# A hybrid mixer's second half in another order, and block products in four column groups

## The reference

```python
def compress_blocks(tok, pos, w1, b1, w2, n_cmp):        # n_cmp = 15
    idx = CMP_STRIDE * jnp.arange(n_cmp)[:, None] + jnp.arange(CMP_BLOCK)[None, :]
    blk = tok[:, idx] + pos[:, None, :]
    blk = blk.transpose(0, 1, 3, 2, 4).reshape(bsz, n_cmp, NSA_KV_GROUPS, CMP_BLOCK * NSA_HEAD_DIM)
    return jax.nn.gelu(blk @ w1 + b1) @ w2               # w1: 2048 x 256, for keys and for values

def hybrid_mixer(h, ...):
    z, xbc, dt_raw, q, k, v, f_raw = jnp.split(h @ w_in, offs, axis=-1)
    xbc = jax.nn.silu(causal_conv(xbc, conv_w, conv_b))
    xs, bm, cm = jnp.split(xbc, ...)
    dt = jax.nn.softplus(dt_raw + dt_bias)
    y = ssd_chunked(xh, dt, -jnp.exp(a_log), bm, cm) + d_skip * xh      # two chunks of 128 tokens
    y = y * jax.nn.silu(z)
    y_ssm = y * lax.rsqrt(mean of y*y per group of 512 + NORM_EPS) * ssm_norm_g
    log_f = jax.nn.log_sigmoid(f_raw + fox_b_f)
    o = forgetting_attention(q, k, v, log_f)                            # 8 heads of 128
    return jnp.concatenate([y_ssm, o], axis=-1) @ w_out
```

## Time and profile before

| | us |
|---|---|
| runs shown | 2211.20, 2202.96, 2211.48; median 2211.2 |
| profiled execution, own time | 2208.97 |
| its span | 2207.5 |
| PE busy | 2122.1 (96%) |
| DVE busy | 1365.1 (62%) |
| ACT busy | 1127.2 (51%) |
| POOL busy | 72.0 (3%) |
| DMA | 369.27 MB, mean 167 GB/s |

### The profile page before, as it was taken

How to read it: one execution, slowest core, us unless ns; L and a number is a source line. 1 busy time by engine, 2 the same in 40 slices (tenths; PEclk the granted TensorE clock), 3 DMA queues, 4 the chain that set the end, 5 groups by cost and what they waited for, 6 DMA issues and landing times.

```text
span 2207.5 us, 25418 instructions
## 1 busy us (share of the span) xinstructions
PE 2122.1 (96%) x9936; PEld 1736.3 (79%) x9936; DVE 1365.1 (62%) x1948; ACT 1127.2 (51%) x1818; POOL 72.0 (3%) x106
## 2 busy tenths in 40 slices
PE   8999899999999989999999999979999999999998
PEld 6877787888887778788788877658788788877887
DVE  5977655554797665555465447665655655577553
ACT  5547455443555546544454446534544544377442
POOL 0000100000000200000000000100000000010000
PEclk9999999999999999999999999989999999999999
DMA  6562353555555234345455544313555555544453
GB/s 236 193 216 89 121 181 122 189 187 177 189 191 191 80 131 154 139 184 191 172 189 184 190 181 172 129 43 115 193 181 189 190 183 189 190 177 165 178 187 133
DMA packets 52950, 369.27 MB, mean 167 GB/s; under 512 B 6207, under 2 KB 6463, under 8 KB 9312
## 3 DMA queue, kind: packets, MB, share of 16 engines
q1 hardware_dynamic: 49104, 356.54, 44.7%
q10 hardware_dynamic: 3216, 9.53, 1.4%
q0 software_dynamic: 512, 1.57, 0.4%
HBM read 366.31 MB, written 1.31 MB: 167 GB/s over the span
## 4 chain that ended last, share of the span: by engine, by line
PE 86%; DVE 6%; ACT 5%; issue 1%; DMA 0%; POOL 0%; ACTq 0%; DVEq 0%
PE ps L481 25%; PE ps L483 25%; PE ps L482 25%; PE ps L569 2%; DVE nT_lo L1243 2%; PE ps L620 1%; DVE ring_lo L1181 1%; PE ps L742 1%; PE ps L553 1%; PE ps L604 1%; ACT nT_hi L1975 1%; ACT upper_w L1911 1%; ACT ostage L1963 1%; PE ps L821 1%; PE ps L539 1%
## 5 line engine op out<-in xcount | busy, mean ns | idle before, releaser
L482 PE MATMUL ps<-ring_lo,nT_hi 128*128 128x512 f32 x1952 | 764.2, 392 | 0.0
L1181 DVE TENSOR_TENSOR ring_lo<-ring,upper_w 128x1024 fp32r<-128x1024 f32 x443 | 536.1, 1231 | 279.7 <-ACT upper_w L1911 276.9
L1911 ACT CAST upper_w<-ring 128x1024 fp32r<-128x1024 f32 x443 | 456.2, 1056 | 340.7 <-PE ps L483 170.8
L481 PE MATMUL ps<-upper_w,nT_hi 128*128 128x512 f32 (+1 forms) x1352 | 540.5, 400 | 19.0 <-DVE ring_lo L1181 11.5
L483 PE MATMUL ps<-upper_w,nT_lo 128*128 128x512 f32 (+1 forms) x1224 | 478.8, 391 | 0.0
L482 PEld LDWEIGHTS ps<-ring_lo,nT_hi 128*128 128x128 f32 x1952 | 370.9, 190 | 73.3 <-issue 0.5
L481 PEld LDWEIGHTS ps<-upper_w,nT_hi 128*128 128x128 f32 x1352 | 257.6, 191 | 78.6 <-issue 9.5
L483 PEld LDWEIGHTS ps<-upper_w,nT_lo 128*128 128x128 f32 x1224 | 232.1, 190 | 49.1
L482 PE MATMUL ps<-ring_lo,z_hi 128*128 128x512 f32 x624 | 242.9, 389 | 0.0
L483 PE MATMUL ps<-upper_w,tT_lo 128*128 128x512 f32 (+1 forms) x528 | 206.8, 392 | 0.0
L1181 DVE TENSOR_TENSOR ring_lo<-ring,PT_w 128x1024 fp32r<-128x1024 f32 x108 | 129.5, 1223 | 73.8 <-ACT PT_w L1911 73.1
(11 more groups left out here) (330 smaller groups left out, 2492.5 us busy)
## 6 DMA issues: line engine op xcount, KB each, us to landing
ring<-in_w SPq DMA_DIRECT2D x339, 1024.0 KB, 4.8
big<-in_gains ACTq DMA_DIRECT2D x7, 512.0 KB, 4.7
z<-in_mem ACTq DMA_DIRECT2D x2, 1024.0 KB, 5.1
big<-skew POOLq DMA_DIRECT2D x8, 192.0 KB, 7.0
x<-in_x SPq DMA_DIRECT2D x2, 512.0 KB, 4.9
xn<-in_w ACTq DMA_DIRECT2D x1, 1024.0 KB, 10.7
out<-x ACTq DMA_DIRECT2D x2, 512.0 KB, 2.7
const<-in_const ACTq DMA_DIRECT2D x1, 529.0 KB, 3.5
```

Source lines behind the costliest of these rows:

```text
L481: PE.matmul(out, hi, w_hi, start=start, stop=False)
L482: PE.matmul(out, hi, w_lo, start=False, stop=False)
L1181: V.tensor_tensor(ring_lo[:, q % RING, cols], ring[:, q % RING, cols], upper(n).bitcast(F32), ALU.subtract).then_inc(*lo_cut.up(h))
L1911: A.copy(upper(n), ring[:, q % RING, part * HALF:(part + 1) * HALF]).then_inc(*hi_cut.up(h))
```

## The change

- The four cmp chunks are no longer one segment behind in5: one is taken behind in3, one behind in4, two behind in5. In each the 8 matmuls go in turn to partitions 0, 32, 64 and 96 of bank 6, so four partial sums stand in four groups of 30 partitions, from four groups of columns of the array. ACT copies all 128 rows; `hidden` sums the groups with a stationary side of K = 128 and a moving matrix `fold` that DVE makes once a layer.
- The mean moves behind `block_scores`, the variance behind the last half of in6, taps 25 to 30 into the front and the halves of in6, the scaling into in7; ACT's Square and Sqrt move with them, and its copy of hid ahead of the scaling of in5.
- In the hybrid mixer x2 goes to banks 6, 7; the turn of the inputs is laid behind the first half of z0 and uses four banks; ACT's Exp of the step sizes goes ahead of its copies. Silu of z moves from behind z3 to behind z2. `to_rows` uses banks 6, 7, 5.
- Q and K of head group 0 are transposed in z7; those of group 1 with `within(1)` between the scores of fox0 and fox1. Key terms 0 come before the weighings on DVE, key terms 1 on POOL. Banks and buffers of y, S0, Q and K change so.
- ACT takes the squares of y in two pairs and scales the two groups of the first token tile, DVE those of the second. y is transposed behind fox0's value products through banks 0 to 3. The first three halves of out0 are laid behind fox1, fox2 and fox3; the transposes of the heads come behind them. All of fox's transposed weights are copied by ACT (`by_act`).

```diff
+CMP_AT = {3: (0,), 4: (1,), 5: (2, 3)}
...
+            for piece in CMP_AT.get(b, ()):
+                w.add(f"{l}.cmp{piece}", [at + 24 + piece], split=False)
         w.end_run(f"{l - 1}.in{LAST[0]}" if l else "0.in0", f"{l}.in{FIRST[-1]}")
-        w.add(f"{l}.cmp", range(at + 24, at + 28), split=False)
...
-    hid = S[0:30, 0, 0:2, :]
+    hid, fold = S[:, 0, 0:2, :], S[:, 1, 1, 0:30]
...
-    y_banks = ((5, 6), (4, 7))
+    key_banks = ((4, 5), (6, 7))
+    y_banks = ((6, 7), (4, 5))
...
-    row_sets = ((0, 4), (4, 4), (8, 2))
+    row_sets, row_banks = ((0, 4), (4, 4), (8, 2)), (6, 7, 5)
...
-            rows_in(3, (2, 3), {0: blocks})
-            rows_in(4, (0, 1))
-            rows_in(5, (2, 3))
...
+            def block_product(piece):
+                kind, cc = piece // 2, piece % 2
+                if piece == 0:
+                    PE.wait_ge(*dve_out.at(f"{l}.b.2"))
+                    free(6)
+                h = W.span[f"{l}.cmp{piece}"][0]
+                q = W.halves[h][0]
+                PE.wait_ge(*landed[q % RING].at(q))
+                w = ring[:, q % RING, :]
+                for j in range(8):
+                    o = 32 * (j % 4)
+                    m = PE.matmul(ps[o:o + 30, 6, kind * 256:(kind + 1) * 256], cmpb[:, kind, 8 * cc + j, :, :].rearrange("p g c -> p (g c)"),
+                                  w[:, j * 256:(j + 1) * 256], start=(cc == 0 and j < 4), stop=(cc == 1 and j >= 4))
+                    if j % 4 == 3:
+                        m.then_inc(*half_used.up(h + j // 4))
+
+            rows_in(3, (2, 3), {0: blocks})
+            block_product(0)
+            rows_in(4, (0, 1))
+            block_product(1)
+            rows_in(5, (2, 3))
+            block_product(2)
+            block_product(3)
...
-                        m = PE.matmul(ps[:, 7, o:o + 30], hid[:, kind, ht * P:(ht + 1) * P], ident[0:30, 0:30], start=True, stop=True)
+                        m = PE.matmul(ps[:, 7, o:o + 30], hid[:, kind, ht * P:(ht + 1) * P], fold, start=True, stop=True)
...
-            rows_in(6, (0, 1), {0: hidden, 1: lambda: (block_rows(), variance()), 2: block_scores})
+            rows_in(6, (0, 1), {0: hidden, 1: block_rows, 2: lambda: (block_scores(), mean()), 3: variance})
...
+                banks = (2 * b, 2 * b + 1) if b < 2 else (6, 7)
...
+                turn("hyb.cin", cols_of(z, H_X), 12, [act_out.at("hyb.x2")], lambda c: act_out.at(f"hyb.cin.{c}"), banks=(6, 7, 4, 5))
...
+                gemm(f"hyb.z{b}", lhs, banks, beside=lambda c: inputs() if b == 0 and c == 0 else None)
...
-                    b = 6 + (3 * t + q) % 2
+                    b = row_banks[q]
...
+                PE.wait_ge(*(pool_out if hg else dve_out).at(f"hyb.terms{hg}"))
+                free(*key_banks[hg])
...
-            work = {0: sums, 2: lambda: to_rows(0), 3: lambda: row_sums(0), 5: lambda: to_rows(1), 7: products, 8: lambda: row_sums(1), 15: lambda: key_sums(0)}
+                held(dve_out.at(f"hyb.added{hg}"), *key_banks[hg])
+
+            def queries(hg):
+                turn(f"hyb.Q{hg}", cols_of(z, H_Q + 512 * hg), 4, [act_out.at(f"hyb.z{2 + hg}")], lambda c: act_out.at(f"hyb.Q{hg}.{c}"))
+
+            def keys(hg):
+                turn(f"hyb.K{hg}", cols_of(z, H_K + 512 * hg), 4, [act_out.at(f"hyb.z{4 + hg}")], lambda c: act_out.at(f"hyb.K{hg}.{c}"))
+
+            work = {0: sums, 2: lambda: to_rows(0), 3: lambda: row_sums(0), 5: lambda: to_rows(1), 7: products, 8: lambda: row_sums(1),
+                    12: lambda: queries(0), 13: lambda: keys(0), 15: lambda: key_sums(0)}
...
-            within(1)
-
-            for hg in range(2):
-                turn(f"hyb.Q{hg}", cols_of(z, H_Q + 512 * hg), 4, [act_out.at("hyb.z7")] if hg == 0 else (), lambda c: act_out.at(f"hyb.Q{hg}.{c}"))
-                turn(f"hyb.K{hg}", cols_of(z, H_K + 512 * hg), 4, (), lambda c: act_out.at(f"hyb.K{hg}.{c}"))
-            key_sums(1)
...
+            def second_tokens():
+                within(1)
+                queries(1)
...
+            def out_halves(first, last):
+                for c in range(first, last):
+                    h = W.span["hyb.out0"][c]
+                    w_hi, w_lo = weights(h)
+                    for k in range(2):
+                        f, cols = 2 * c + k, slice(k * BLK, (k + 1) * BLK)
+                        PE.wait_ge(*dve_out.at(f"hyb.yT.lo{f}" if f < 8 else f"hyb.hT.lo{f - 8}"))
+                        for t in range(TT):
+                            m = three(ps[:, 2 * t, :], pair_hi(f, TOK[t]), wide_lo(f, TOK[t]), w_hi[:, cols], w_lo[:, cols], f == 0, f == 15)
+                    m.then_inc(*half_used.up(h))
+
+            def y_product():
+                free(0, 2)
+                out_halves(0, 1)
+            attention(fox_units(), scores, lambda i: [act_out.at(f"hyb.K{i // 2}.2"), act_out.at(f"hyb.Q{i // 2}.2")], between=second_tokens, first=lambda: key_sums(1), by_act=True,
+                      beside={0: lambda: parts("hyb.yT", cols_of(z), 8, lambda c: [act_out.at("hyb.ynorm"), dve_out.at("hyb.ynorm")], (0, 1, 2, 3)), 1: y_product, 2: lambda: out_halves(1, 2)})
+            out_halves(2, 3)
+            parts("hyb.hT", lambda c, t: heads_out[c // 4][t][:, c % 4 * P:(c % 4 + 1) * P], 8, lambda c: [dve_out.at("fox3.out")])
+            out_halves(3, 8)
...
+                if n == 0:
+                    V.tensor_reduce(fold, ident.rearrange("p (q i) -> p i q", q=4)[:, 0:30, :], AX_X, ALU.add).then_inc(*dve_out.up(f"{l}.fold"))
...
-            cuts(f"{l}.in5", lambda n: tap(22 + n))
...
+            cuts(f"{l}.in5", lambda n: tap(22 + n) if n < 3 else None)
+            cut_first(f"{l}.in6", 1)
+            tap(25)
+            cut_first(f"{l}.in6", 2)
+            tap(26)
+            tap(27)
+
+            def centre():
...
-            work = {1: lambda: (block_keys(), deviation()), 2: block_scores, 3: lambda: (scaled(), block_weights())}
-            cuts(f"{l}.in6", lambda n: work.get(n, lambda: None)())
-            cuts(f"{l}.in7", lambda n: block_values() if n == 3 else None)
+            work = {0: lambda: tap(28), 1: lambda: (block_keys(), tap(29), tap(30)), 2: lambda: (block_scores(), centre()), 3: lambda: (block_weights(), deviation())}
+            cuts(f"{l}.in6", lambda n: work[n]())
+            late = {0: scaled, 3: block_values}
+            cuts(f"{l}.in7", lambda n: late.get(n, lambda: None)())
...
-                    11: lambda: weigh(0), 12: lambda: weigh(1), 13: lambda: key_terms(0)}
+                    11: key_terms, 12: lambda: weigh(0), 13: lambda: weigh(1)}
...
+            def second_tokens():
+                V.wait_ge(*pool_out.at("hyb.dx1"))
+                own()
...
                 mean_square("hyb.y", 4, 512, 0)
...
+            def y_parts():
                 V.wait_ge(*pool_out.at("hyb.y.rstd"))
-                for i, s in enumerate(groups):
-                    V.tensor_scalar(s, s, st[:, i:i + 1], None, ALU.mult).then_inc(*dve_out.up("hyb.ynorm" if i == 3 else None))
-            attention(fox_units(), plain_out, first=y_norm, beside={1: lambda: lo_parts("hyb.yT", 8, (pair_hi, wide_lo), s2("ng"))})
-
-            def heads_beside(n):
-                if n == 2:
-                    lo_parts("hyb.hT", 8, ((lambda c: pair_hi(8 + c)), (lambda c: wide_lo(8 + c))))
-            cuts("hyb.out0", heads_beside)
+                for i in (2, 3):
+                    V.tensor_scalar(groups[i], groups[i], st[:, i:i + 1], None, ALU.mult).then_inc(*dve_out.up("hyb.ynorm" if i == 3 else None))
+            attention(fox_units(), plain_out, between=second_tokens, first=y_norm, by_act=True, amid={1: y_parts},
+                      beside={0: lambda: lo_parts("hyb.yT", 8, (pair_hi, wide_lo), s2("ng"), (0, 1, 2, 3)), 1: lambda: cut_ahead(span[0]), 2: lambda: cut_ahead(span[1])})
+            cut_ahead(span[2])
+            lo_parts("hyb.hT", 8, ((lambda c: pair_hi(8 + c)), (lambda c: wide_lo(8 + c))))
+            for h in span[3:]:
+                cut_ahead(h)
             for h in W.span["hyb.out1"][:-2]:
                 cut_ahead(h)
...
+            cuts(f"{l}.in5")
+            cut_first(f"{l}.in6", 2)
+            A.wait_ge(*product(f"{l}.cmp3"))
+            A.copy(hid, ps[:, 6, :].rearrange("p (k n) -> p k n", k=2)).then_inc(*act_out.up(f"{l}.hid"))
+            scaled(f"{l}.in5", block_of(z, 3), ps[:, 2:4, :], func=ACT.Sigmoid)
...
+            cut_to(W.halves[W.span[f"{l}.in6"][2]][2])
+            hidden()
+            rows_in(6, 0, block_of(z, 4), ACT.Sigmoid, {1: block_rows, 3: lambda: (squared(), block_weights())})
+            rows_in(7, 2, block_of(z, 5), ACT.Sigmoid, {0: deviation, 1: normed, 2: weights_turned})
...
-                scaled(f"hyb.x{b}", block_of(z, 2 + b), ps[:, 2 * (b % 2):2 * (b % 2) + 2, :])
+                bank = (0, 2, 6)[b]
...
             A.wait_ge(*dve_out.at("hyb.sp"))
             e = acc[:, 3, 0:56]
```

(35 more changed lines are left out.)

127 lines of the change are left out of this document (43 added, 84 removed).

## The result

The changed kernel takes 2174.6 us (median of four runs, 2172.6 to 2176.4) where the kernel before takes 2207.1 beside it: a ratio of 0.986 (95% interval 0.983 to 0.988). In a second comparison the two stood at 2174.6 and 2205.9, ratio 0.985 (0.983 to 0.988). The forecast was 2183 us, range 2172 to 2198. In the profiled executions the span fell from 2207.5 to 2171.1 us, by 36.4, more than the 28.1 of the sum; the medians of the runs differ by 32.5 and 31.2.

What follows compares the result with a forecast made beforehand. TensorE was taken as the bound (86% of the chain that ended last), VectorE next. Savings of 1.9 + 5.2 + 11.6 + 9.4 = 28.1 us from 2208.97 gave 2180.9, plus 2.2 for the median: 2183 us, range 2172 to 2198.

Steps and rivals of the forecast that it cites:

- A: Turning the hybrid mixer's inputs, laid behind the first products of z0: saves 1.9 us (bounds 0.5 and 2.5).
- B: z4 to z7 of the hybrid mixer: waits and half clock go, some wait returns; saves 5.2 us (bounds 2.0 and 7.2).
- C: End of z7 to the first output product: less idle and low clock; saves 11.6 us (bounds 5 and 18).
- D: Block products of both layers, in four column groups at once: saves 9.4 us (bounds 0 and 13).
- The walk through the queues: Tail behind z7: following four engine queues with old durations found 5.0 us of PE waits, taken as 7.
- my walk: Input projection: layer 0 followed step by step with PE's waits; 5.5 us saved a layer at 1.0 us a chunk.
- Column groups in turn: Rival for the block products: the groups do not run at once and gain nothing; 2192 us, chance 0.14.
- Loads that alternate with products: Rival for the block products: load and product take turns, 5.3 us a chunk; 2206 us, chance 0.03.
- C at half its gain: Rival for the tail behind z7: its serial chain shows again between the output halves; 2189 us, chance 0.16.
- the tail at half clock: Rival: PE, cut into short bursts, stays at half clock over the whole tail; 2220 us, chance 0.02.
- Rival 5: Whole kernel better than forecast, down to 2172 us, with the bounds at their good end; chance 0.05.

Runs made afterwards that it cites:

- before_again: The kernel before, unchanged, run once more for a second trace: 2206.9 us.
- triangle_later: The changed kernel with the second row sums asked for one half of products later: 2168.3 us, ratio 0.983.
- front_only: The kernel before with the input projection's part of the change alone: 2192.7 us, against 2201.0 for the kernel before beside it.
- hybrid_only: The kernel before with the hybrid mixer's part of the change alone: 2179.8 us, against 2201.0 for the kernel before beside it.
- second_first: The changed kernel with the second tokens put ahead of the first unit's scores on all engines: 2170.1 us.
- halves_behind: The changed kernel with the first three output halves behind the attention instead of between its steps: 2172.7 us.
- one_group: The changed kernel with all block products in one column group again, places kept: 2189.4 us.
- two_and_pairs: The changed kernel with layer 0's block products in two column groups, layer 1's in four with two in a row to each: 2178.0 us, one run.

## Why the prediction came out right, point by point

| step | forecast | profiled | what was off |
|---|---|---|---|
| A | 1.9 | 2.6 | the 24 transposes took 3.9 us, now 2.8 |
| B | 5.2 | 3.8 | half clock behind the new wait |
| C | 11.6 | 17.3 | low clock: 8.7 returned, not 3.2 |
| D | 9.4 | 7.8 | more saved, more waited |
| elsewhere | 0 | 4.9 | layer 0's half clock, its start |
| sum | 28.1 | 36.4 | |

A is read from the start of x0 to the sums (82.0 and 79.4 us), B from there to the end of z7 (59.9 and 57.9, less 1.8 for 16 transposes that have moved in), C from there to the transposes behind the output product (104.7 and 85.6, with the 1.8), D as P of both layers (3.4 and 4.4). Of the 4.9 elsewhere, 3.5 lie between P of layer 0 and P of layer 1, where before_again also takes 3.6 us less than the first trace of before: they are not the change's. The steps themselves gave 31.5 us.

**A.** The waits of 1.4 us and 0.5 us went as put down. I left the transposes at their cost, but a break for a bank costs more than its idle time, which the profile counts only from the end of the last record (0.27 us long). Their starts stand 0.109 us apart, and across the two breaks 0.57 and 0.46 us, where the idle times are 0.30 and 0.19. From the first transpose to the next product it was 3.63 us and is 2.53: 1.1 us less, of which 0.5 was in the sum. The clock had no part in it: it was 1.00 there (1331 to 1337 us) in the kernel before.

**B.** All waits went where the step had them, and the one that was to come did: 1.91 us for the second triangle, put down as 2.0. What failed is one term: I added 1.7 us for the half clock behind the old wait and charged none behind the new one. It was 1.8 us (5.40 for eight records of 3.59). With it the sum is 3.4. triangle_later confirms both halves of that loss, and shows that it could have been had for one number in a table.

**C.** The walk through the queues gave 7 us of waits, the trace has 6.8, though not the same ones. K1 waited 1.9 and not 0.6, as I had overlooked the squares of y that ACT does ahead of the copies. POOL's terms took 4.8 us (I took 5) and nobody waited for them. The scaled rows cost 1.3 and not 2.4 (the row for L572 names DVE's L1336, but that ended at 1456.90; ACT's scaling, L2392, ended at 1457.75, and PE went on at 1457.85). The first output half cost 1.5 for the parts of y and not 0.9 for a bank. The longest wait, 2.0 us ahead of the second unit's transposes, had not been seen. It has the same cause as K1's: its probabilities were ready at 1450.66, but the first unit's had to leave the banks, and ACT copies them only behind the second pair of squares:

```profile
1451.51 0.63 ACT L2375 ACTIVATE tT<-z 128x512 f32<-128x512 f32 x1
1452.13 0.56 ACT L2076 COPY PTs<-ps 128x512 f32<-128x512 f32 x1
```

The idle part is 8.6 by the forecast's 15.4 against 6.8, as counted (8.4). The clock is the mis-sized term: I put down 5.7 us lost before and 2.5 after. Before it was 8.7, by what is left of C's 17.3 without the idle part, and after it is nil (clock 1.00). Not in my list were both groups of L1031 (4.57 and 4.49 against 3.68) and some tenths in each of the other groups. The mean clock of 0.83 over 61 us gave the warning: worked out as in step B, it is some 21 us at half clock and up to 10 us lost. front_only shows that 3.4 us of this belong to how the tail happened to be met, so a fair size for C is 14 to 17 (an estimate from these two numbers). hybrid_only (H 232.8) shows that the whole of it comes with the hybrid part. Within it the halves were tested, 0.5 us, and they don't hold the clock up; which step brought the clock back stays open. That the idle time went because the key terms come ahead of the weighings, and because ACT took squares, scalings and the copies of the probabilities over from DVE, fits the waits that are gone, but no run shows it: second_first and halves_behind only rule out two other steps.

**D.** The products fell to 0.97 us a chunk, below my lower bound of 1.1 and my value of 1.4, so PE work fell by 10.1 us a layer and not 8.6 (the 0.97 is half of the 1.93 us of two chunks in a row). I had taken the bound from records of another kind and not from the simplest ratio, a quarter of the pitch. The waits behind were right in kind and nearly in size (keys 1.2 for 1.6, last tap 1.25 for 1.3, squares none for 0.8), but behind the wait for the tap the mean's products ran at half clock (3.5 us in layer 1 for 2.0), and a cut and the convolution's parts add 0.5 to 0.9. Layer 0 also waits 0.8 us for the block inputs ahead of the first chunk. At 1.0 us a chunk my walk had given 5.5 us a layer; 3.4 and 4.4 were measured. Here too the clock behind a wait was the missing term, and with it the switches between narrow and full products, below.

**The rivals.** Column groups in turn (2192) is refuted by one_group and two_and_pairs. Loads that alternate with products (2206) too: 14.3 us for 64 records in one group, 0.216 us from start to start, leave no room for loads of 0.1 us each. The Trainium skill, page "TensorE: Matmul & The Clock Gate", section "The mechanism", has a list by which loads overlap running products only where their row groups differ; by that sentence they should not have been hidden, as all use all rows, and the trace doesn't agree. The same section also lets a load be taken ahead into a background weight buffer; that would fit, and no run here tests it.

The prediction also passed over the drain at a change of tiling mode, which the Trainium skill states (page "TensorEngine Tiling (Array Packing)", section "Key Properties"), because the row of L742 has no idle before it. The idle column doesn't show it, but the starts do. Here is one chunk between full products in the changed kernel, then eight full products of the same 256 columns (L761) between the same neighbours:

```profile
119.60 0.39 PE L486 MATMUL ps<-upper_w,nT_lo 128*128 128x512 f32 x1
119.92 1.07 PE L743 MATMUL ps<-ring,PTs 128*30 128x256 f32 x16
120.92 0.50 PE L484 MATMUL ps<-upper_w,nT_hi 128*128 128x512 f32 x1
121.25 0.39 PE L485 MATMUL ps<-ring_lo,nT_hi 128*128 128x512 f32 x1
```

```profile
156.06 0.39 PE L486 MATMUL ps<-upper_w,nT_lo 128*128 128x512 f32 x1
156.29 1.89 PE L761 MATMUL ps<-cbuf,const 128*128 128x256 f32 x8
157.82 0.58 PE L484 MATMUL ps<-upper_w,nT_hi 128*128 128x512 f32 x1
158.24 0.40 PE L485 MATMUL ps<-ring_lo,nT_hi 128*128 128x512 f32 x1
```

Into the narrow products it is 0.32 us where 0.23 is usual. From the first of them to the second full one behind it is 1.33 us, where four distances of 0.216 and one of 0.227 make 1.09. For L761 it is 1.95 us, just eight of 0.216 and one of 0.227. So a switch there and back costs some 0.3 us here. The trace thus agrees with the page. The layer has three such pairs, and before the change it had two and not one, as the mean stood between chunks 3 and 4: the change adds some 0.3 us a layer (an estimate from these starts).

C at half its gain (2189) did not happen, nor the tail at half clock (2220): its clock is 1.00. Rival 5, the good end of the bounds (2172), had a chance of 0.05, and the measured 2174.6 lies nearer to it than to the forecast of 2183, because C came out near its upper bound of 18.

**The measured time** lies 8.4 us below the forecast. Half of that is the start: I counted from a median of 2211.2, and the kernel before took 2207.1 in this comparison. The gain is 32.5 us for 28.1. It is that near partly by luck, since errors of both signs met: C's clock (5.5 us) and D's products (1.5 us a layer) gave more than I put down, and the clock behind two new waits, which I had put at nothing, took some of it back.

## What to carry to other kernels

Put down each wait of PE with two prices, the idle time and the slower records behind it; here 1.9 us of idle brought 1.8 us of half clock, and both went by asking for the result one half later. Where several small products with a narrow stationary side stand in a row, spread them over column groups: less than a third of the time (4.1 us for 14.3), and one number to undo. Read what a switch or a break costs from the starts of the records and not from the idle column. And before crediting the most visible step of a change, move it back alone: here the interleaved halves were worth 0.5 us.

## What the runs showed of the chip that was not expected

- Products of 30 stationary columns and 256 moving ones in float32: 14.3, 7.5 and 4.1 us for 64 records in one, two and four column groups, four starting within 0.02 us of each other. Two in a row to the same group cost nothing (4.2), and products pass each other there: the 8th record of the program starts as the 14th.
- A switch from full products to products of 30 columns and back costs some 0.3 us (0.09 going in, 0.24 coming out), which no idle time shows.
- Idle time doesn't always bring half clock. A gap of 1.91 us before the second row sums did each time; gaps of 1.9, 2.05, 1.3 and 1.5 us in the same kernel's tail, spread over 20 us, did not (clock 1.00).
- One program has different half-clock stretches in different executions, in layer 0 and between layer 1 and the hybrid mixer above all: the same 30 us stretch at a clock of 1.00 and 0.89, for the kernel before and for the changed one alike.
